# RWKV pairs of a two-block kernel: the small transposes of the first 16 tokens move from TensorE and ScalarE to VectorE

## The reference, cut to what matters

```
sa = einsum('bhij,bhj->bhi', S, a_t)
S  = S * w_t[:, :, None, :] + sa[..., None] * b_t[:, :, None, :] + v_t[..., None] * k_t[:, :, None, :]
y  = einsum('bhij,bhj->bhi', S, r_t)
```

## Time and profile before

| | |
|---|---|
| median of 3 runs | 1478.48 us (1478.38 to 1480.16) |
| profiled execution | 1479.58 us, span 1477.8 us |
| PE busy | 1445.4 us, 98% of the span, 10956 instructions |
| PEld busy | 1318.6 us, 89% |
| DVE busy | 1024.4 us, 69%, 1962 instructions |
| ACT busy | 907.4 us, 61%, 2127 instructions |
| POOL busy | 59.1 us, 4% |
| granted TensorE clock | 0.999 of full speed |
| chain that ended last | PE 81%, DVE 11%, ACT 6%, issue 2% |

### The profile page before, as it was taken

The page is one execution under the profiler, slowest core; times in us unless marked ns, Lnnn a source line. Parts: engine busy times, 40 slices in busy tenths (PEclk is TensorE's granted clock), DMA queues, the critical chain, the costliest instruction groups (busy, mean ns, idle before and its releaser), DMA issues.

```text
span 1477.8 us, 27893 instructions
## 1 busy us (share of the span) xinstructions
PE 1445.4 (98%) x10956; PEld 1318.6 (89%) x10956; DVE 1024.4 (69%) x1962; ACT 907.4 (61%) x2127; POOL 59.1 (4%) x30
## 2 busy tenths in 40 slices
PE   9999999999999999998999999999999999999997
PEld 8898988888999999897898989898989899799986
DVE  4468686656698875887777777777777547567764
ACT  4457667755567764476666666666666546566653
POOL 1343100000000000000000000000000000000000
PEclk9999999999999999999999999999999999999999
DMA  9464543222545555242101110111011136333340
GB/s 354 173 209 139 196 154 104 86 86 86 183 160 195 177 171 187 99 146 84 52 36 59 58 59 29 58 58 58 29 59 58 47 126 236 121 115 115 115 143 29
DMA packets 26465, 171.71 MB, mean 116 GB/s; under 512 B 3776, under 2 KB 5216, under 8 KB 6496
## 3 DMA queue, kind: packets, MB, share of 16 engines
q1 hardware_dynamic: 25152, 168.81, 32.6%
q10 hardware_dynamic: 1184, 1.11, 0.2%
HBM read 168.84 MB, written 1.08 MB: 115 GB/s over the span
## 4 chain that ended last, share of the span: by engine, by line
PE 81%; DVE 11%; ACT 6%; issue 2%; DVEq 0%; ACTq 0%
PE bank L785 10%; PE bank L786 10%; PE bank L787 9%; PE bank L1159 3%; PE bank L1328 3%; PE bank L1344 3%; PE bank L769 2%; PE bank L1160 2%; PE bank L1179 2%; PE bank L1161 2%; DVE ring L2891 2%; PE bank L967 2%; PE bank L1321 1%; DVE sd L2773 1%; PE bank L1255 1%
## 5 line engine op out<-in xcount | busy, mean ns | idle before, releaser
L685 DVE TENSOR_TENSOR ring_lo<-ring,w_hi 128x1024 fp32r<-128x1024 f32 x122 | 149.8, 1231 | 94.1 <-ACT w_hi L1601 93.1
L685 DVE TENSOR_TENSOR ring_lo<-ring,w_hi_rw 128x1024 fp32r<-128x1024 f32 x126 | 153.6, 1221 | 46.9 <-ACT w_hi_rw L1601 45.7
L1601 ACT ACTIVATE w_hi<-ring 128x1024 fp32r<-128x1024 f32 x144 | 151.9, 1057 | 29.1 <-PE bank L787 14.3
L1601 ACT ACTIVATE w_hi_rw<-ring 128x1024 fp32r<-128x1024 f32 x126 | 132.4, 1053 | 37.9 <-PE bank L1518 15.7
L1569 ACT ACTIVATE arena<-bank 128x272 f32<-128x272 f32 (+3 forms) x173 | 70.0, 406 | 110.8 <-PE bank L787 49.6
L1159 PE MATMUL bank<-x_hi,w_hi_rw 128*128 128x272 f32 x384 | 130.7, 340 | 0.9
L1160 PE MATMUL bank<-x_lo,w_hi_rw 128*128 128x272 f32 x384 | 111.0, 289 | 0.0
L1161 PE MATMUL bank<-x_hi,ring_lo 128*128 128x272 f32 x384 | 111.0, 289 | 0.0
L785 PE MATMUL bank<-u_hi,w_hi 128*128 128x256 f32 x320 | 90.0, 281 | 1.5 <-DVE ring_lo L685 1.5
L787 PE MATMUL bank<-u_hi,ring_lo 128*128 128x256 f32 x320 | 89.7, 280 | 0.0
L786 PE MATMUL bank<-u_lo,w_hi 128*128 128x256 f32 x320 | 89.6, 280 | 0.0
(11 more groups left out here) (523 smaller groups left out, 4560.2 us busy)
## 6 DMA issues: line engine op xcount, KB each, us to landing
ring<-wstream SPq DMA_DIRECT2D x151, 1024.0 KB, 4.9
arena<-spread_norms SPq DMA_DIRECT2D x1, 2048.0 KB, 7.1
con<-consts SPq DMA_DIRECT2D x1, 2024.0 KB, 13.8
h<-xT SPq DMA_DIRECT2D x1, 1024.0 KB, 6.0
sq<-spread SPq DMA_DIRECT2D x1, 1024.0 KB, 4.3
arena<-spread SPq DMA_DIRECT2D x2, 512.0 KB, 6.0
arena<-wlora ACTq DMA_DIRECT2D x1, 1024.0 KB, 9.0
out<-arena SPq DMA_DIRECT2D x4, 256.0 KB, 2.1
```

The source lines that it names most:

```text
L685: ops.tensor_tensor(lo, whole, hi.bitcast(F32), ALU.subtract).then_inc(S(signal), 1)
L1601: nc.scalar.activation(hi, whole, ACT.Copy).then_inc(S("w_hi_ready"), 1)
```

## The change

Chunk 0's turned gram is no longer computed. VectorE transposes a 32x32 block of the plain gram straight out of banks 5 and 6 into `A20` (which gets 32 columns a head), each transpose right ahead of the instruction that masks the same gram into `G0`. ScalarE's two copies to `A20` and the wait behind them go; `rw_turned_taken` now counts one for a pair. In the three short levels TensorE's transpose of the small inverse and ScalarE's copy to `T0` go; VectorE transposes the 32x32 block of `U0w` straight into `T0`, ahead of its wait for y.

```
-        A20 = uf[:, 1952:1984].rearrange("p (a b) -> p a b", a=2)
+        A20 = uf[:, 1888:1952].rearrange("p (a b) -> p a b", a=2)
...
             def turned_grams(p):
-                for c in (1, 2, 0):
+                for c in (1, 2):
                     t0, n = RCH[c]
-                    at = (320, 0, P)[c]
+                    at = (0, P)[c - 1]
...
                 pe.wait_ge(S("rw_grams_taken"), 3 * p + 3)
-                pe.wait_ge(S("rw_turned_taken"), 3 * p + 3)
+                pe.wait_ge(S("rw_turned_taken"), p + 1)
...
-                    if short:
-                        ins = nc.tensor.transpose(bank[3][:, 2 * P:3 * P], U0w[:, l % 2, 0:P], C("ident"))
                     ins.then_inc(S("rw_t"), 1)
...
                 act.wait_ge(S("rw_grams_taken"), 3 * p + 3)
-                for j in range(2):
-                    nc.scalar.activation(A20[0:META, j, :], bank[5 + j][0:META, 320:320 + META], ACT.Copy).then_inc(S("rw_turned_taken"), 1)
-                act.wait_ge(S("rw_turned_taken"), 3 * p + 3)
                 for l in range(1, 4):
                     nc.scalar.activation(A20p[0:META, META * (l - 1):META * l].rearrange("p (m b s) -> p m b s", m=2, s=1 << l),
-                                         parts(A20[0:META], l, 0), ACT.Copy)
+                                         parts(A20[0:META, :, 0:META], l, 0), ACT.Copy)
...
                     act.wait_ge(S("rw_t"), 6 * p + l)
-                    if l < 4:
-                        nc.scalar.activation(T0[:, 0:META], bank[3][:, 2 * P:2 * P + META], ACT.Copy)
...
                     if c == 0:
-                        dve.wait_ge(S("rw_turned_taken"), 3 * p + 1)
+                        dve.wait_ge(S("rw_turned_taken"), p + 1)
                     for j in range(2):
                         if c == 0:
+                            V_.transpose(A20[0:32, j, :], bank[5 + j][0:32, 256:288])
                             ins = V_.tensor_tensor(G0[0:n, p % 2, j, :], bank[5 + j][0:n, 256:256 + 4 * n], C("mask_rw0", 4 * n, n), ALU.mult)
...
                 for l in range(1, LEVELS):
+                    if l < 4:
+                        dve.wait_ge(S("rw_step"), 7 * p + l)
+                        if l >= 2:
+                            dve.wait_ge(S("rw_even"), 6 * p + l - 1)
+                        V_.transpose(T0[0:32, 0:32], U0w[0:32, l % 2, 0:32])
                     dve.wait_ge(S("rw_y"), 6 * p + l)
```

## The result

The changed kernel takes 1471.88 us (median of 6 runs, 1471.64 to 1472.35), against 1478.67 us for the kernel before beside it (6 runs, 1478.38 to 1480.16): 6.8 us less, ratio 0.995 with a 95% interval of 0.994 to 0.996. The forecast was 5.4 us less (1473.1 us). The mechanism came out as forecast, one term did not.

A forecast was written before the change was run, and what follows sets the result against it. A loop per pair over TensorE's levels, VectorE's masks, ScalarE and L1222 was taken to bound the kernel. Terms 5.2 + 0.2 + 0 = 5.4 us off the 1478.48 us median gave 1473.1 us, range 1471.5 to 1476.9 us.

The forecast's parts named there:

- What bounds the kernel: Each middle pair is a 31.50 us loop: L1222, TensorE through the levels, VectorE's masks, ScalarE's copies and pack, L1222.
- The small inverse's transposes: Levels 1 to 3: 48 TensorE transposes at 0.11 us go, VectorE's replacements nearly free; 5.2 us off.
- Chunk 0's turned gram: Two of L1216's six matmuls go, 0.1 us; counts only in pairs 0 and 1, 0.2 us off.
- the forecast's cap: At L1222: were t nearly nothing, the loop would gain no more than TensorE's 0.13 us wait.
- The exchange at chunk 0's masks: ScalarE loses 0.27 us a pair, VectorE gains two transposes of 0.27 us together; even over 14 pairs, 0 us.
- t: Time one VectorE transpose adds at chunk 0's masks, taken as 0.136 us; between 0.10 and 0.18 us: chance 0.68.
- Rival 1: At chunk 0's masks, transposes don't overlap with masks, t = 0.27 us; 1476.9 us, chance 0.13 with what lies towards it.
- Rival 2: In the levels, another wait takes back TensorE's saving; 1478.3 us if all is taken back, chance 0.07.
- Rival 3: At chunk 0's masks, a VectorE transpose is slow, t = 0.43 us; slower than before, 1481.4 us, chance 0.05.
- Rival 4: More than forecast: t = 0.09 us at chunk 0's masks, 1471.8 us; 1471.5 with larger turned-gram saving; chance 0.07.
- What would show it: Trace signs: L1222 distance 31.17 us, transposes and masks 0.61 us, first pack unchanged from L2895, no wait at L1344.

The follow-up runs named there:

- e3: Changed kernel with two more VectorE transposes at chunk 0's masks, into unused columns: 1475.46 us.
- e8: Changed kernel with ScalarE's pack(p, 1) moved ahead of its wait for chunk 0's masks: 1469.22 us.
- e1: Kernel before with only the levels' part of the change, T0 by VectorE's transpose, small turned gram kept: 1473.55 us.
- e5: Changed kernel with TensorE's 48 small transposes L1324 still issued, result unused: 1476.91 us.
- e6: Changed kernel with chunk 0's two small turned matmuls of a pair still issued, result unused: 1472.15 us.
- e7: Changed kernel with four VectorE transposes in place of one ahead of the small y in levels 1 to 3: 1472.10 us.
- e9: Changed kernel with the edits of e8 and e6 together, pack moved and two small turned matmuls still issued: 1471.52 us.
- e2: Changed kernel with the levels as before, leaving only the gram's part, A20 by VectorE's transposes: 1477.80 us.
- e4: Changed kernel with two additional plain copies of the same 32x32 blocks on VectorE at chunk 0's masks: 1475.15 us.
- e10: Kernel before with only ScalarE's pack(p, 1) moved ahead of its wait for chunk 0's masks: 1478.25 us.
- e11: Changed kernel timed once more, unedited, beside others on the same chip: 1472.66 us.

## Why the prediction was right or wrong, point by point

**What bounds the kernel.** Right. The loop L1222, TensorE, VectorE, ScalarE, L1222 is there before and after. e3 (an addition on VectorE's part: +0.19 us a pair), e8 (an instruction moved out of ScalarE's part: the wait goes) and e1 with e5 (TensorE's part, both signs) each touch one arc of it and move the time; e6 and e7 touch what lies off it and leave the middle pairs as they are.

**The small inverse's transposes, 5.2 us.** Right: 5.5 us done alone, 5.0 us undone alone. The price was the distance of starts, 0.11 us, and not the duration, 0.27, which would have given 13 us. VectorE's replacements cost nothing, and would have had room for three more each (e7).

**Chunk 0's turned gram, nothing but in pairs 0 and 1.** The mechanism is shown by e6: nothing in the middle pairs. The size was 0.14 us in place of 0.1, and the last pair counts too (0.12 us), where the forecast had nothing. e9 shows the condition: without the wait at L1222 the two count in every pair. For the same reason the forecast's cap on what the loop can gain beyond the levels, the 0.13 us of the wait, is too low: two matmuls fewer add their 0.14 us to the wait, and e8 takes 0.28 us beyond the levels' 0.33 (31.50 to 30.89, medians of the middle distances).

**The exchange at chunk 0's masks, 14 x (0.27 - 0.27) = 0.** This is the step that failed, in its size. ScalarE's 0.27 us was right. t was not 0.136 us but 0.19 / 2 = 0.095 us, close to the lower bound that I took from the 16-element instruction. So the term is 14 x (0.27 - 0.19) = 1.1 us, and with the 0.24 us of the two matmuls in the first and the last distance the gram's part comes to 1.3 us, which e2 measured with an interval of 0 to 2.5 us. That, and not the levels, is the bulk of the 1.4 us between the forecast and the measurement. I had taken t from the mask's 64 elements by nearness of place, and priced the transpose as if the mask behind it stayed as it was. The transpose itself was near my price (0.13 us to the mask's start); the mask then ends 0.035 us sooner, 0.17 us after its start where masks in a row take 0.204. Why it does is open. My reason that fewer elements and the turning of the block would cancel finds no support in e4: a plain copy in the same place moves the masks' end by the same 0.10 us.

**Rival 1 (no overlap)** is excluded: a transpose lasts 0.20 us and the next instruction starts 0.13 us behind it, or 0.10 behind one that follows another. The rule of the Trainium skill (VectorE: DVE Perf Modes, "The DRAIN you can't avoid"), that the next instruction starts when the pipe is empty, is not what these rows show, for transposes as little as for masks. The same section adds that a next instruction starts earlier where it is not held back, which the prediction left out; these rows are such a case (0.13 us between starts, 0.20 us of duration). **Rival 2** is excluded by e1, e5 and e7. **Rival 3** had its turning point at t = 0.33 us, far above the 0.095 measured. **Rival 4** is what happened: it gave 1471.8 us for t = 0.09 us. Of the signs under "What would show it", the four instructions at the masks took 0.53 us and not 0.61, and the first pack came 0.08 us closer to the large mask in place of at the same distance; the others came out.

In the trace the time between the first and the last pair's L1222 (682.90 to 1155.29 before, 682.24 to 1147.79 after) shrank by 6.8 us: 12 middle pairs of 0.42 us, 0.4 us for the first, 0.8 for the second, 0.6 for the last. Behind the last one its own levels add 0.3 us. So the profiled pair of executions shows 7.2 us for the change, the medians 6.8. The second distance explains it. In the kernel before, level 6's mask of pair 1 starts late, 0.51 us idle where the later ones have 0.16 or less, and with it the rest of VectorE's part; pair 2's copies to A20 end at 743.32 us, and TensorE waits for them at chunk 1's to_tokens until 743.44:

```profile
733.42 0.42 DVE L2909 TENSOR_TENSOR u<-bank,con 128x256 f32<-128x256 f32 x1 [0.51 <-PE bank L1328]
743.44 0.30 PEld L1222 LDWEIGHTS bank<-con,arena 128*128 128x128 f32 x2 [0.25 <-issue]
```

The changed kernel has neither. But that is not the change's doing: e1, which still has ScalarE's copies, has no wait there either (its second distance is 31.15 us, as its others) and has the same late mask in another place, at 950.64 us with 0.51 us idle and a distance of 31.51; behind it TensorE waits at the same step, 0.35 us between the loads (960.30 to 960.65). e10, whose VectorE does the same as in the kernel before, has it in pair 1 again (0.50 us idle). Without these 0.35 us the traces show 6.9 us, as the medians do. What makes the mask late is open.

## What to carry to other kernels

In a loop over engines, price an edit by the arc that it lies on: the same two matmuls were worth nothing while TensorE had to wait for ScalarE later in the loop, and 0.15 us a pair once that wait was gone. A removal and an addition that seem to cancel on the critical arc deserve the sharper price, since the result is their difference times the number of rounds; price an inserted instruction by how far it moves the end of the group that the next engine waits for, not by its duration, and remember that the instruction behind it can get shorter. And look at what the engine with the last word does between the release and its signal: whatever needs no release can go ahead of the wait.

## What the runs showed of the hardware

A 32x32 fp32 transpose on VectorE lasts 0.19 to 0.20 us out of PSUM or SBUF (after), and 0.16 us when another transpose of the same block precedes it (e3). The next small instruction starts 0.13 us behind it, or 0.10 behind a second one. An added one moved the end of the masks by 0.10 us, and so did a copy of the block (e4). A 16x64 mask lasts 0.20 us behind another mask or a copy (before, e4) and 0.17 us behind a transpose (after, e3). On TensorE a fp32 transpose of 128x128 costs 0.11 us of the stream (e1, e5), and the two 64-row matmuls of 16 columns together 0.14 to 0.15 us (e6, e9), with a granted clock of 1.00 from 745 to 1150 us in all of these traces. In e11 a dip to 0.79 of the clock between 698 and 706 us went with 1.4 us more from pair 0 to pair 1.
